# Quarter products for the forget-gate and value projections inside the gated scan

## The chip, the cores and the metric

The kernel runs on one core of a Trainium2 chip. The metric is the device time of one execution in microseconds (us), the median over runs. TensorE is called PE here, VectorE DVE, ScalarE ACT, GpSimd POOL; SP is the engine whose queue issues most of the transfers.

## The reference, cut to what matters

Two transformer blocks run one after the other. The second one (the suffix `_2` in the weights) projects 256 context tokens and 256 latent tokens with `w_in_2`, runs a gated linear scan over 8 heads in two directions, and attention beside it:

```python
b = jnp.cumsum(log_f, axis=3)                 # in chunks of 32 tokens
k_inv, q_dec = k * jnp.exp(-b), q * jnp.exp(b)
kv_chunk = einsum('bhnsk,bhnsv->bhnkv', k * jnp.exp(b_last - b), v)
S = decay * S + kv_chunk                      # from chunk to chunk
o = tril(q_dec k_inv^T) v + q_dec S
```

A forget gate is a sigmoid of a projection of all 512 tokens by 128 columns of `w_in_2` (one set for each head and each direction), scaled into a lower bound; k is one minus the gate. The value of a head is a projection of all 512 tokens by 128 columns, without a function. Query and output gate are needed for the 256 latent tokens only.

## The kernel before, in words

Everything is float32, and each matmul of the source is two matmul instructions in the trace. The stages that matter are `in_projection2` (the input norm and the projections of heads 0 and 1), `hgrn` (the scan of all heads, and the projections of heads 2 to 7 and of attention beside it), and `attention`.

**Weights** come through a ring of three slots of 2 MB (2048 x 256 columns). SP issues the loads strictly in the order of the list `SLOTS`; load n waits until slot n-3 is given back (`issue`, L338). In `hgrn` nine slots make a group (the slots are counted from the stage's first): f0, mod, f1, mod, q, mod, i, mod, g. f0 and f1 hold the gate columns of the two directions for two heads, i the value columns, and mod is a slice of `w_mod_2`, which DVE, not PE, multiplies (`mod_macs`, L661 to L672: 16 instructions and one add) and gives back at its end. One mod slot is used in each step u = 0 to 13: slots 1, 3, 5, 7, 10, 12, 14, 16, 19 and so on.

**The scan** has 16 steps u (head u//2, direction u%2). In each, PE writes the chunk products (L2835; the moment it starts is called kv(u) below), DVE carries the state through them in 15 dependent instructions (`carry_state`, L3065 and L3067), and PE reads the later states (L2843, then eight times L2848). DVE then forms the sums of step u+1 (L3028 to L3036), ACT their exponentials (L2923 to L2926), DVE the end keys (L3042), then the 16 instructions of `mod_macs`, then the masked scores (L3047), then the gate of the next step (L3021). PE turns the keys of u+1 (L2806) and makes the scores (L2812).

**Dense work beside the scan.** PE fills its gaps with the projections, a generator of jobs (`MIX2_JOBS`) of which `fill(us)` takes as many matmuls as their written prices make up:

```python
MIX2_FILL = {"carry": 7.0, "step": 0.43, "ahead": 11.0, "keys": 5.0}
```

In one step this is 7.0 after kv(u), seven times 0.43 between the reads of the states, 11.0 after them, and 5.0 after the keys: 26.0 us by the written prices. 14.0 us are taken ahead of step 0. After every fourth step what is left of the group is done at once (`fill_upto`). The written price is 0.856 us for a matmul of 512 columns and 0.428 for one of 256. A group p (1 to 3) has four f jobs (16 matmuls of 512 columns, L2752), two q (16 of 256, L2754), four i (16 of 256, tokens on the partitions, L2750) and two g (as q). Jobs alternate between banks 5 and 7; a job may start when ACT has emptied the one before the last (`W("dense_out", j - 1)`). ACT empties them in `dense_out`, at fixed places in its own list: ahead of `log_gates`, ahead of `exponentials`, ahead of `keys_out`.

`in_projection2` already computes its own f0 and f1 as seven quarter products with sums of tokens (`tok_sum`) and of weights (L2594 to L2599) by DVE.

Of the kernel before, what the change touches and what calls it, by code (L numbers as in the profile page):

```python
# [217 lines left out]
MIX2_FILL = {"carry": 7.0, "step": 0.43, "ahead": 11.0, "keys": 5.0}  # L218
# [1645 lines left out]
def ffn(nc, st, name, which, mods, gain, shift):  # L1864
# [58 lines left out]
    with nc.Block() as block:  # L1923
        @block.sync
        def _(sp):
# [3 lines left out]
            if which == 0:  # L1929
                sp.dma_start(st.const[:, st.const_late:], st.dram["const"][:, st.const_late:]).then_inc(st.s_back, 16)  # L1930
# [480 lines left out]
def in_projection2(nc, st):  # L2411
# [13 lines left out]
    s_tokens, s_wsum, s_seven, s_p1, s_post = (st.sem("in2_" + x) for x in ("token_sums", "weight_sums", "products", "p1", "post"))  # L2425
# [22 lines left out]
    with nc.Block() as block:  # L2448
        @block.sync
        def _(sp):  # L2450
            stream_weights(sp, st, SPANS["mix2"][0] + RING)
# [99 lines left out]
        def _(dve):  # L2551
# [36 lines left out]
            tt(tok_sum[3], tok_sum[1], tokens(1, 0), ALU.subtract).then_inc(s_tokens, 1)  # L2588
# [12 lines left out]
            def post(x):  # L2601
# [12 lines left out]
                vl.mark(tt(fb[:, one], fb[:, two], r[4], ALU.subtract))  # L2614
# [9 lines left out]
            for k in range(KT):  # L2624
                x = st.xT[:, k, :]
                vl.mark(stt(x, x, final[:, k:k + 1], ra, ALU.mult, ALU.mult))
# [9 lines left out]

MIX2 = []
for _g in range(4):
    if _g < 3:
        _p = _g + 1  # L2640
        _jobs = [("f", 4 * _p + _u) for _u in (0, 2, 1, 3)] + [("q", 2 * _p), ("q", 2 * _p + 1)]
        _jobs += [("i", 4 * _p + _t) for _t in range(TT)] + [("g", 2 * _p), ("g", 2 * _p + 1)]
        if _g:
            _jobs.insert(2, ("hn", _g - 1))
# [9 lines left out]
def mix2_slot(job):  # L2654

    kind, i = job
    if kind in ("f", "q", "i", "g"):
        p = {"f": i // 4, "q": i // 2, "i": i // 4, "g": i // 2}[kind]
        return 9 * (p - 1) + {"f": 2 * (i % 2), "q": 4, "i": 6, "g": 8}[kind]
    return {"ak": 27, "aq": (29, 31, 32, 33)[min(i // 2, 3)], "av": 34}[kind]  # L2660

# [5 lines left out]
def hgrn(nc, st):  # L2667
# [42 lines left out]
    norms = [("nk", 0), ("nk", 1)] + [("nq", n) for n in range(4)]  # L2710

# [11 lines left out]
    with nc.Block() as block:  # L2723
        @block.sync
        def _(sp):
            stream_weights(sp, st, SPANS["att"][0] + RING)

        @block.tensor
        def _(pe):
# [4 lines left out]

            def dense():
                nonlocal done
                freed = None
                for j, (kind, i) in enumerate(MIX2_JOBS):
# [3 lines left out]
                    if kind in ("f", "q", "i", "g", "ak", "aq", "av"):  # L2742
# [3 lines left out]
                        half = {"f": i // 2 % 2}.get(kind, i % 2)  # L2746
                        for k in range(KT):
                            if kind in ("i", "av"):
                                t = i % 4
                                last = mm(b[:, 0:256], st.h2[:, t // 2, k, (t % 2) * P:(t % 2 + 1) * P], w[:, k, :], start=k == 0, stop=k == KT - 1)  # L2750
                            elif kind in ("f", "ak"):
# [9 lines left out]
                            yield 0.856 if kind in ("f", "ak") else 0.428  # L2761
# [56 lines left out]
            for u in range(U):  # L2818
# [3 lines left out]
                if h >= 2:  # L2822
                    W("dense_out", mix2_at(("i", h // 2 * 4 + 3)))
# [21 lines left out]
                for n in range(8, 16):  # L2845
# [5 lines left out]
                    if n < 15:  # L2851
                        fill(MIX2_FILL["step"], upto=marks[u, "carry"] + 2)
                fill(MIX2_FILL["ahead"], (u, "ahead"))
# [9 lines left out]
        def _(act):  # L2863
# [5 lines left out]
            def dense_out(upto):  # L2869
# [3 lines left out]
                while n_out < upto:  # L2873
# [3 lines left out]
                    if kind == "f":  # L2877
                        W("kend", i // 4 * 4 - 4)
                        W("qk", 2 * (i // 4 * 4 - 4))
                        ins = a_(fu(i), x[:], ACT.Sigmoid)  # L2880
# [3 lines left out]
                    elif kind == "i":  # L2884
                        W("inter", 8 * (i // 4 * 4 - 4))
                        ins = nc.scalar.copy(st.pi[i // 4 % 2][:, i % 4, :], x[:, 0:256])
# [45 lines left out]

            log_gates(0)
# [3 lines left out]
            for u in range(U):  # L2937
# [3 lines left out]
                dense_out(marks[u, "carry"])  # L2941
                if u + 1 < U:
                    exponentials(u + 1)
# [8 lines left out]
                if u + 1 < U:  # L2952
                    keys_out(u + 1)
            dense_out(J)
# [17 lines left out]
        def _(dve):  # L2972
# [44 lines left out]
            def gates(u):  # L3017
                f, lc = fu(u), 8 * (u % 2) + u // 2
                if u >= 4:
                    W("dense_out", mix2_at(("f", u)))  # L3020
# [375 lines left out]
```

## Time and profile before

| what | value |
|---|---|
| median of 3 runs | 3558.76 us |
| the runs | 3560.2, 3549.15, 3558.76 us |
| span of the profiled execution | 3558.3 us |
| PE busy | 96% of the span |
| DVE, ACT, POOL busy | 66%, 16%, 5% |
| `hgrn` in the trace | about 2042 to 2575 us |

The span runs from the first to the last instruction. The profiled execution's time outside the span is not given; the span lies 0.5 us under the median of the runs. "Idle before" is the time for which an engine stood still just ahead of an instruction, with what released it. Busy time of PE counts overlapping records once, and a mean duration includes the drain, so a price is taken from start to start.

### The profile page before, as it was taken

What the parts mean: (1) busy time and instruction counts of PE and PEld (TensorE: products, weight loads), DVE (VectorE), ACT (ScalarE), POOL (GpSimd) and SP (SyncE); (2) the same over time, 40 slices, a digit from 0 to 9 for tenths busy, and PEclk for the clock granted to TensorE, in tenths of its full rate; (3) what the DMA queues carried; (4) which work ended last, traced back from release to release, by engine and by line L of the source; (5) the groups of instructions that cost most, each with busy time, mean ns of one, the idle gap of its engine ahead of it and who ended that gap; (6) DMA issues with size and microseconds to landing.
All of it is one profiled execution on the core that took longest, in us unless ns stands there. A gap on an engine that the chain in (4) does not pass through costs nothing. (4 is left out here: it accounts for less than half of the span.)

```text
span 3558.3 us, 58548 instructions
## 1 busy us (share of the span) xinstructions
PE 3421.8 (96%) x25037; PEld 2759.0 (78%) x25037; DVE 2336.2 (66%) x4471; ACT 564.2 (16%) x1072; POOL 162.7 (5%) x168
## 2 busy tenths in 40 slices
PE   7998999899999999999999999999999999999999
PEld 4456555577778888889998866767877888888888
DVE  2277877785559888998776645555654656644644
ACT  2232222221001000000002132222221000000000
POOL 1000000000000000000001000000001000000000
PEclk9999999999999999999999999999999999999999
DMA  9833333344587878776665644544324676654543
GB/s 338 259 79 105 104 86 106 106 120 122 191 285 234 263 245 267 237 253 203 212 209 182 205 150 142 166 142 132 120 80 147 222 234 201 221 174 160 178 166 130
DMA packets 663410, 638.48 MB, mean 179 GB/s; under 512 B 43490, under 2 KB 630752, under 8 KB 662128
## 3 DMA queue, kind: packets, MB, share of 16 engines
q1 hardware_dynamic: 554464, 563.16, 49.3%
q10 hardware_dynamic: 108016, 71.44, 6.9%
q8 instruction: 198, 3.24, 0.4%
q14 instruction: 60, 0.49, 0.0%
q0 software_dynamic: 672, 0.15, 0.0%
HBM read 628.41 MB, written 6.29 MB: 178 GB/s over the span
## 5 line engine op out<-in xcount | busy, mean ns | idle before, releaser
L2005 PE MATMUL bank<-work,extra 128*128 128x256 f32 x2112 | 463.1, 379 | 0.0
L664 DVE SCALAR_TENSOR_TENSOR work<-weight_ring,silu_c,work 128x256 f32<-128x256 f32 x1050 | 450.5, 501 | 0.0
L2005 PEld LDWEIGHTS bank<-work,extra 128*128 128x128 f32 x2112 | 401.3, 190 | 53.5
L2005 PE MATMUL bank<-weight_ring,work 128*128 128x256 f32 x1408 | 318.1, 385 | 8.1 <-ACT work L2138 7.5
L2206 DVE TENSOR_TENSOR work<-weight_ring 128x2048 f32<-128x2048 f32 (+2 forms) x72 | 129.7, 1801 | 294.1 <-DMA weight_ring<-in_w_gate_up 160.9
L2005 PEld LDWEIGHTS bank<-weight_ring,work 128*128 128x128 f32 x1408 | 269.8, 193 | 45.5 <-issue 8.3
L1013 PE MATMUL bank<-work,x_channels 128*128 128x256 f32 (+1 forms) x704 | 243.5, 486 | 0.0
L2752 PE MATMUL bank<-work,weight_ring 128*128 128x512 f32 x448 | 203.9, 600 | 1.2 <-PEq L2448 1.2
L1013 PEld LDWEIGHTS bank<-work,x_channels 128*128 128x128 f32 x704 | 129.3, 194 | 75.5 <-issue 63.6
L2005 PE MATMUL bank<-weight_ring,extra 128*128 128x256 f32 x704 | 159.3, 380 | 2.2 <-DVE extra L2201 2.2
L2005 PE MATMUL bank<-work 128*128 128x256 f32 x704 | 159.3, 379 | 0.0
L2754 PE MATMUL bank<-work,weight_ring 128*128 128x256 f32 x640 | 151.0, 386 | 0.7 <-ACT work L2899 0.7
L2005 PEld LDWEIGHTS bank<-weight_ring,extra 128*128 128x128 f32 x704 | 133.8, 190 | 20.8 <-issue 2.9
L2752 PEld LDWEIGHTS bank<-work,weight_ring 128*128 128x128 f32 x448 | 81.4, 191 | 86.6 <-issue 84.4
L2217 DVE TENSOR_TENSOR work<-weight_ring,work 128x2048 f32<-128x2048 f32 (+2 forms) x72 | 129.8, 1803 | 27.8 <-PE bank L2005 19.1
L2005 PEld LDWEIGHTS bank<-work 128*128 128x128 f32 x704 | 130.7, 190 | 15.8
L2213 DVE TENSOR_TENSOR work<-work,weight_ring 128x2048 f32<-128x2048 f32 (+2 forms) x72 | 129.4, 1798 | 14.4 <-PE bank L2005 11.4
L2754 PEld LDWEIGHTS bank<-work,weight_ring 128*128 128x128 f32 x640 | 117.8, 190 | 20.9 <-ACT work L2899 4.4
L2209 DVE TENSOR_TENSOR work<-weight_ring 128x2048 f32<-128x2048 f32 (+2 forms) x72 | 129.4, 1797 | 3.4 <-PE bank L2054 2.6
L3067 DVE SCALAR_TENSOR_TENSOR extra<-extra,work,bank 128x128 f32<-128x128 f32 x224 | 77.9, 348 | 78.7 <-PE bank L2848 72.7
L1676 DVE SCALAR_TENSOR_TENSOR const<-weight_ring,silu_c,const 128x256 f32<-128x256 f32 x240 | 116.1, 484 | 18.7 <-DMA weight_ring<-in_w_mod 12.7
L2074 PE MATMUL bank<-work,weight_ring 128*128 128x128 f32 x1056 | 124.6, 276 | 1.7 <-DVE work L2201 1.6
(463 smaller groups left out, 5481.9 us busy)
## 6 DMA issues: line engine op xcount, KB each, us to landing
weight_ring<-in_w_mod SPq DMA_DIRECT2D x80, 2048.0 KB, 9.9
weight_ring<-in_w_gate_up SPq DMA_DIRECT2D x44, 2048.0 KB, 9.4
weight_ring<-in_w_in SPq DMA_DIRECT2D x26, 2048.0 KB, 9.3
weight_ring<-in_w_gate SPq DMA_DIRECT2D x22, 2048.0 KB, 8.3
weight_ring<-in_w_up SPq DMA_DIRECT2D x22, 2048.0 KB, 13.0
weight_ring<-in_w_down SPq DMA_DIRECT2D x20, 2048.0 KB, 8.1
weight_ring<-in_w_mod ACTq DMA_DIRECT2D x32, 1024.0 KB, 6.7
weight_ring<-in_w_out SPq DMA_DIRECT2D x16, 2048.0 KB, 10.2
```

The source lines that it names most:

```text
L664: ins = v_.scalar_tensor_tensor(a, w[:, k, :], c, a, ALU.mult, ALU.add)
L1013: last = mm(b[:, 0:TA if both else T], w[:, k, :], x, start=k == 0, stop=k == KT - 1, skip_group_check=j == 0)
L1676: ins = v_.scalar_tensor_tensor(acc, mod_half[:, k, :], x, acc, ALU.mult, ALU.add)
L2005: last = mm(product(u, p), right[p][:, k, :], left[p][:, k, :], start=k == 0, stop=k == 7)
L2074: last = mm(product2(u, p), left[p][:, k, :], right[p][:, k, :], start=s == 0 and k == 0 and j % 4 == 0, stop=s == 3 and k == hi - lo - 1, ...
L2206: tt(out[0], a21, a22, ALU.add).then_inc(st.s_sum, 1)
L2209: tt(out[1], a11, a21, ALU.subtract).then_inc(st.s_sum, 1)
L2213: tt(out[2], out[0], a11, ALU.subtract).then_inc(st.s_sum, 1)
L2217: tt(out[3], a12, out[2], ALU.subtract).then_inc(st.s_sum, 1)
L2752: last = mm(pair(b[:]), w[:, k, half * P:(half + 1) * P], st.h2[:, :, k, :], start=k == 0, stop=k == KT - 1)
L2754: last = mm(b[:, 0:T], w[:, k, half * P:(half + 1) * P], st.h2[:, 1, k, :], start=k == 0, stop=k == KT - 1)
L3067: v_.scalar_tensor_tensor(where(n + 1), where(n), D[:, u % 2, g:g + 1], kv, ALU.mult, ALU.add).then_inc(S("state"), 1)
```

## The change

The f0, f1 and i slots of groups 1 to 3 (nine slots) are computed as seven products of quarters: the 2048 input channels are halved, and so are the columns (the two heads) and the tokens (context, latent). Each product is 8 matmuls of 256 columns for f (56 a slot, where there were 32 of 512) and 16 of 128 columns for i (112 a slot, where there were 64 of 256). They accumulate in PSUM in the turn 1, 2, 6, 7, 5, 4, 3; ACT empties the bank after each, and DVE adds three kept quarters (`seven_post`). DVE makes four sums of weight quarters a slot, two of them in place in the ring slot (`seven_sums`, `seven_last_sum`). The sigmoid of three of the four quarters is taken later (`open_gates`).

The sums of tokens that the products need are kept from `in_projection2`. Two of them are copied into the place of the residual `xT`, which is written to DRAM before (2 MB) and read back near the end of `hgrn`. So the 16 instructions that scale the residual (L2626) move ahead of the first weight sums, and SP in `in_projection2` waits for the write. A late part of the constants (0.59 MB), loaded at the start of the first feed-forward stage before, is loaded late in `hgrn`. The fill after the states is 9.5 instead of 11.0 in steps 0 to 11, and the limit on the fills between the states goes.

```diff
-MIX2_FILL = {"carry": 7.0, "step": 0.43, "ahead": 11.0, "keys": 5.0}
+MIX2_FILL = {"carry": 7.0, "step": 0.43, "ahead": 9.5, "late": 11.0, "keys": 5.0}
# ffn, SP
-            if which == 0:
-                sp.dma_start(st.const[:, st.const_late:], ...).then_inc(st.s_back, 16)
# in_projection2, SP
+            stream_weights(sp, st, first + 5)
+            sp.wait_ge(s_final, KT)
+            sp.dma_start(st.x_kept, st.xT...).then_inc(st.s_kept, 16)
+            sp.wait_ge(s_tokens, 4)
+            sp.wait_ge(st.s_kept, 32)
+            for j in range(2):
+                sp.dma_start(st.ts_kept[2 + j]..., tok_sum[2 + j]...).then_inc(st.s_tokens_kept, 16)
             stream_weights(sp, st, SPANS["mix2"][0] + RING)
# in_projection2, DVE, ahead of weight_sums(2)
+            for k in range(KT):
+                x = st.xT[:, k, :]
+                stt(x, x, final[:, k:k + 1], ra, ALU.mult, ALU.mult).then_inc(s_final, 1)
# jobs of a group
-        _jobs = [("f", 4 * _p + _u) for _u in (0, 2, 1, 3)] + [("q", 2 * _p), ("q", 2 * _p + 1)]
-        _jobs += [("i", 4 * _p + _t) for _t in range(TT)] + [("g", 2 * _p), ("g", 2 * _p + 1)]
+        _jobs = _seven[0] + ([("hn", _g - 1)] if _g else []) + _seven[1] + [("q", 2 * _p), ("q", 2 * _p + 1)]
+        _jobs += _seven[2] + [("g", 2 * _p), ("g", 2 * _p + 1)]
# hgrn, SP
+            stream_weights(sp, st, first + 28)
+            sp.wait_ge(S("dense_mm"), seven_at(len(SEVENS) - 1, 3))
+            sp.dma_start(st.const[:, st.const_late:], ...).then_inc(st.s_back, 16)
+            sp.dma_start(st.xT..., st.x_kept).then_inc(st.s_x_home, 16)
# hgrn, PE
+            def seven_product(i, b):
+                s, j = i // 7, i % 7
+                p = SEVEN_TURN[j]
...
+                if p == 6:
+                    W("weight_sums", 4 * s + 3)
+                    pe.wait_ge(st.s_tokens_kept, 32)
+                if p == 3:
+                    W("weight_sums", 4 * s + 4)
...
+                if SEVENS[s][1] != "i":
+                    for k in range(8):
+                        yield mm(out, left[:, k, :], right[:, k, :], ...), k == 7, 0.432
+                    return
+                for t in range(2):
+                    for k in range(8):
+                        yield (mm(out[:, t * P:t * P + P], right[:, k, t * P:t * P + P], left[:, k, :], ...), k + t == 8, 0.224)
# hgrn, DVE
+            def seven_sums(s):
+                a11, a12, a21, a22 = quads(s)
+                arrived(dve, st, first + mix2_slot(("s", 7 * s)))
+                if s:
+                    W("dense_mm", seven_at(s - 1, 5))
+                tt(s1, a21, a22, ALU.add).then_inc(S("weight_sums"), 1)
+                tt(a21, a11, a21, ALU.subtract).then_inc(S("weight_sums"), 1)
+                W("weight_sums", 4 * s + 1)
+                tt(s2, s1, a11, ALU.subtract).then_inc(S("weight_sums"), 1)
...
             gates(0)
             sums(0)
             end_keys(0)
+            seven(marks[-1, "ahead"], 0)
             scores_out(0)
             for u in range(U):
                 if u + 1 < U:
                     gates(u + 1)
+                seven(marks[u, "steps"], marks[u - 1, "keys"])
                 carry_state(u)
                 if u + 1 < U:
                     sums(u + 1)
                     end_keys(u + 1)
+                    seven(marks[u, "ahead"], marks[u, "steps"])
                     if u < MIX2_MODS:
                         mod_macs(...)
                     scores_out(u + 1)
+                    seven(marks[u, "keys"], marks[u, "ahead"] - 1)
+                    if u == 12:
+                        dve.wait_ge(st.s_back, 32)
# hgrn, ACT: a further dense_out(marks[u, "steps"]) ahead of exponentials(u + 1), and
+                if u in (2, 6, 10):
+                    open_gates(u // 4 + 1)
# attention, DVE, ahead of the first use of xT
+                    dve.wait_ge(st.s_x_home, 16)
```

`seven(begun, reached)` makes the three sums of a slot as soon as its product 6 is at most three jobs behind `begun`, the last sum by the same rule for product 3, and the three additions once product 4 is at or below `reached`; `marks` are the numbers of jobs that PE has finished at a point of its list.

## Rows read from the trace of the kernel before

**Rows 1.** The page: the span, and busy us (share) and instructions by engine.
```profile
span 3558.3 us, 58548 instructions
PE 3421.8 (96%) x25037; PEld 2759.0 (78%) x25037; DVE 2336.2 (66%) x4471; ACT 564.2 (16%) x1072; POOL 162.7 (5%) x168
```
**Rows 2.** Windows: stretch, length, then busy us (instructions) by engine, clock, DMA share, GB/s.
```profile
1932.00:1936.00 4.00, 4.00 (x11) 3.11 (x10) 3.50 (x9) 4.00 (x12) 3.92 (x1) 0.50 0.00 0
2042.00:2575.00 533.00, 530.84 (x2646) 381.21 (x2646) 298.66 (x635) 152.97 (x244) 40.61 (x48) 1.00 0.44 142
```
**Rows 3.** Groups by line, 2042 to 2575 us: busy us, mean ns, idle before.
```profile
L2752 PE MATMUL bank<-work,weight_ring 128*128 128x512 f32 x448 | 203.9, 600 | 1.2 <-PEq L2448 1.2
```
**Rows 4.** Timeline of PE: start, us, line, operands, count; 256-, 512- and 128-column runs.
```profile
1972.39 13.98 PE L2471 MATMUL bank<-work 128*128 128x256 f32 x64
1986.20 0.50 PE L690 MATMUL bank<-const 128*128 128x1 f32 x4
...
2042.73 13.11 PE L2752 MATMUL bank<-work,weight_ring 128*128 128x512 f32 x30 [1.20 <-PEq L2448]
2055.68 0.60 PE L2806 MATMUL bank<-const,work 128*128 128x128 f32 x4
...
1632.44 5.52 PE L2074 MATMUL bank<-work 128*128 128x128 f32 x48
1637.80 2.84 PE L2074 MATMUL bank<-work,weight_ring 128*128 128x128 f32 x24
```
**Rows 5.** Timeline of DVE in `in_projection2`.
```profile
1961.38 1.22 DVE L2594 TENSOR_TENSOR work<-weight_ring 128x1024 f32<-128x1024 f32 x1
...
1964.90 1.23 DVE L2599 TENSOR_TENSOR work<-weight_ring,work 128x1024 f32<-128x1024 f32 x1
...
1972.23 0.43 DVE L672 TENSOR_TENSOR const<-const 128x256 f32<-128x256 f32 x1
1981.95 1.22 DVE L2594 TENSOR_TENSOR work<-weight_ring 128x1024 f32<-128x1024 f32 x1 [9.29 <-DMA weight_ring<-in_w_in]
...
...
2002.37 6.41 DVE L2626 SCALAR_TENSOR_TENSOR x_channels<-x_channels,params,work 128x256 f32<-128x256 f32 x16
```
**Rows 6.** Timeline of SP: load issues in `in_projection2` and `hgrn`.
```profile
1972.68 0.37 SPq L349 DMA_DIRECT2D weight_ring<-in_w_in  x1
...
2111.60 0.37 SPq L349 DMA_DIRECT2D weight_ring<-in_w_in  x1
...
2142.82 13.48 SPq L349 DMA_DIRECT2D weight_ring<-in_w_in  x2
```
**Rows 7.** DMA issues by line, 2040 to 2600 us: count, KB, median us to landing.
```profile
weight_ring<-in_w_in SPq DMA_DIRECT2D x20, 2048.0 KB, 8.6
```
**Rows 8.** Timeline of PE in `hgrn`: kv(1), kv(2), the state reads (first row: `in_projection2`).
```profile
1986.57 7.15 PE L2471 MATMUL bank<-work,weight_ring 128*128 128x256 f32 x32
...
2088.55 1.17 PE L2835 MATMUL bank<-work,extra 32*128 32x128 f32 x32
2119.55 1.17 PE L2835 MATMUL bank<-work,extra 32*128 32x128 f32 x32
2127.67 0.61 PE L2843 MATMUL bank<-extra,work 128*128 128x128 f32 x4
```
**Rows 9.** Timelines of `hgrn`: end keys, state carry, PE's long fill, ACT behind the exponentials.
```profile
2048.52 0.69 DVE L3042 TENSOR_TENSOR work<-work 128x512 f32<-128x512 f32 x1 [1.49 <-ACT work L2926]
2276.34 3.80 DVE L3067 SCALAR_TENSOR_TENSOR extra<-extra,work,bank 128x128 f32<-128x128 f32 x10
...
2257.41 11.47 PE L2750 MATMUL bank<-weight_ring,work 128*128 128x256 f32 x52
2259.60 1.28 ACT L2883 ACT_TABLE_LOAD   x1
2260.89 0.38 ACT L2883 ACTIVATE work<-bank 128x256 f32<-128x256 f32 x1
```
**Rows 10.** Timeline of PE where it starts again after an idle time.
```profile
1930.24 8.26 PE L2495 MATMUL bank<-weight_ring,work 128*128 128x256 f32 x24 [4.53 <-ACT work L2532]
```

More of the change, by code:

```diff
@@ L2613, in post @@
                 vl.mark(tt(fa[:, two], fa[:, two], r[3], ALU.add))
-                vl.mark(tt(fb[:, one], fb[:, two], r[4], ALU.subtract))
+                vl.mark(tt(fb[:, one], fb[:, two], r[4], ALU.add))
                 vl.wait()
@@ L2634, in _ @@
             side.collect(dve)
+SEVEN_TURN = (1, 2, 6, 7, 5, 4, 3)
+SEVENS = [(p, kind) for p in (1, 2, 3) for kind in ("f0", "f1", "i")]
 MIX2 = []
@@ L2741, in dense @@
                     b = bank[5 + 2 * (j % 2)]
-                    if kind in ("f", "q", "i", "g", "ak", "aq", "av"):
+                    if kind == "s":
+                        s = mix2_slot((kind, i))
+                        arrived(pe, st, first + s)
+                        for last, end, took in seven_product(i, b):
+                            if freed is not None:
+                                last.then_inc(st.s_slot_used, 1)
+                                freed = None
+                            if end:
+                                last.then_inc(S("dense_mm"), 1)
+                                done = j + 1
+                            yield took
+                        if i % 7 == 6:
+                            freed = s
+                    elif kind in ("q", "g", "ak", "aq", "av"):
                         s = mix2_slot((kind, i))
@@ L2851, in _ @@
                     if n < 15:
-                        fill(MIX2_FILL["step"], upto=marks[u, "carry"] + 2)
-                fill(MIX2_FILL["ahead"], (u, "ahead"))
+                        fill(MIX2_FILL["step"])
+                marks[u, "steps"] = done
+                fill(MIX2_FILL["ahead" if u < 12 else "late"], (u, "ahead"))
                 if u % 4 == 3:
@@ L2931, in keys_out, with open_gates @@
                 nc.scalar.copy(keT, bank[4][:].rearrange("p (a b) -> p a b", a=TT)).then_inc(S("keT_out"), 1)
+            def open_gates(p):
+                for s in (3 * p - 3, 3 * p - 2):
+                    W("post", s + 1)
+                    x = quarter(s, 0, 0)
+                    a_(x, x, ACT.Sigmoid)
+                    x = st.pf[p % 2][:, 2 + s % 3, :]
+                    a_(x, x, ACT.Sigmoid).then_inc(S("opened"), 1)
+            act.wait_ge(st.s_tokens_kept, 32)
             log_gates(0)
@@ L2941, in _ @@
                 dense_out(marks[u, "carry"])
+                dense_out(marks[u, "steps"])
                 if u + 1 < U:
@@ L3313, in program @@
         st.c = c
+        st.const_span = lambda name, n: st.const[:, const_where[name][0]:const_where[name][0] + n]
         def carve(at, *shape):
@@ L3333, in program @@
         st.lbs = carve(29120, 4, 16)
+        kept_x = st.xT.rearrange("p k t -> p (k t)")
+        st.ts_kept = [x.rearrange("p (a b) -> p a b", a=8) for x in (
+            st.work[:, 16384:18432], st.work[:, 18432:20480], kept_x[:, 0:2048], kept_x[:, 2048:4096])]
         st.squares = st.extra[:, 3072:4096].rearrange("p (m f t) -> p m f t", m=2, f=2)
```

120 lines of the change are left out of this document (92 added, 28 removed).

## The prediction

> **What bounds the kernel now.** I read the page first: PE is busy for 3421.8 of 3558.3 us, so what shortens PE's list shortens the kernel unless a wait takes its place [rows 1]. The windows then tell where the change lies: from 2042 to 2575 us PE is busy for 530.8 of 533 us at full clock, DVE for 298.7 and ACT for 153.0, and the transfers use 44% of the DMA engines [rows 2]. The stage is PE's, without a gap that matters; the two others have room, but the room is worth something only at the right moment. The groups by line name the work: the gate products alone are 448 instructions of 512 columns (224 matmuls), with 1.2 us idle ahead of them [rows 3]. The last view is the timeline, for what a sum of busy time doesn't show: when each slot is given back, when its successor lands, and when PE asks for it.
>
> **Prices.** From start to start an instruction of 256 columns takes 13.81/64 = 0.2158 us, so a matmul 0.4316; of 512 columns 12.95/30 = 0.4317, so 0.863; of 128 columns 5.36/48 = 0.1117, so 0.2233 [rows 4].
>
> **1. What PE saves.** Six f slots: 32 x 0.863 = 27.6 before, 56 x 0.4316 = 24.2 after, 3.4 each, 20.7 in all. Three i slots: 64 x 0.4316 = 27.6 before, 112 x 0.2233 = 25.0 after, 2.6 each, 7.8. Sum **-28.5 us**. The 128-column rows come from a stream in which every instruction has its own load of 128x128 weights, as in the new i product, so I take that price as it is. Its bounds are near: half of the 256-column price below (24.2 us a slot, 0.8 less), and the price of 256 columns above, which the rival on weight loads takes up.
>
> The Trainium skill speaks against the i half. Its page "TensorE: Matmul & The Clock Gate", section "Back-to-back issue gap", says that in a stream of weight loads and matmuls the spacing at 128 columns is set by both, about 81 ns where 56 would be the stream alone, a factor of 1.45. By that rule the i slot would cost 224 x 0.1079 x 1.45 = 35.0 us (estimate), and the sum would be 30 us worse. The trace disagrees: 0.1117 is 1.04 times half of 0.2158 [rows 4].
>
> **2. What DVE gets.** Three sums of 128x1024 take 3.5 us from 1961.38 to 1964.90 [rows 5]; with the fourth and three additions of some 0.4 it is 5.8 us a slot, 52 in nine. DVE has 234 us free in the stage [rows 2], so the amount is hidden. Where it stands is not: three places below.
>
> **3. in_projection2.** The 16 scalings (6.4 us, L2626) move ahead of weight_sums(2). PE asks for sum 5 at 1972.4 and the sum would be ready at 1969.0, so that is hidden. But the mod slot behind it is given back 6.4 us later, and SP issued load first+4 on that release, at 1972.68 [rows 5, 6]. It landed at 1981.95, 9.3 us later; now 1988.4, and PE asks at 1986.57 [rows 8]: **+1.9**. SP then waits for the write of the residual, and the two copies and loads first+5 and first+6 queue behind it. By 8.6 us for 2 MB [rows 7] in a row, first+6 lands at some 2014: 1992.7 for the write, then three times 2 MB at 6.5 to 8.6; PE asks at 2013, seven products of 3.45 behind 1988.5. If everything stands in line at 8.6, it is 6 us late. I take **+1.0**, range 0 to 6. The reload and the constants late in the stage lie behind the last i slot and are asked for 25 us later: 0, and up to 2 if they push load 29. Taking the constants out of the first feed-forward stage gains nothing that a wait of PE shows.
>
> **4. Start of hgrn.** PE starts at 2042.73 and has products 1 and 2 done at 2049.7. Product 6 needs three sums, which DVE puts after end_keys(0), ending at 2049.2 [rows 9]; they end at 2052.7: **+3.0**. In step 0 the sums of the second slot wait for product 5 of the first, which PE does 4 us after kv(0), and they stand ahead of carry_state(0): they end at +7.7, the eighth state is there at +10.7 (8 x 0.38 [rows 9]), and PE asks at 8.1 + 0.6 = +8.7 [rows 8]: **+2.0**.
>
> **5. The slot that PE reaches too early.** This is the step that decides. Slot 6 (i) follows mod slot 3 in the ring, which DVE gives back at the end of mod_macs(1): SP issued it at 2111.60, kv(1) + 23.05 [rows 6, 8]. Before, PE came to it late enough: by written prices 14 + 2 x 26 = 66 us are taken ahead of kv(2), and 4 x 13.7 + 13.7 = 68.5 lie ahead of i. After, a step takes 24.51 us, 63.0 ahead of kv(2), and 14 x 3.456 + 13.7 = 62.1 lie ahead of i: PE comes to it 0.9 us before the end of step 1's fill. Step 1 is 31.0 - 1.5 (ahead) - 0.3 (512-column matmuls ran 1% over their written price) = 29.2 long, 0.5 of its end are the four modulation columns (as the four of [rows 4]), so PE asks at kv(1) + 27.8. DVE's additions push mod_macs(1) by 1.1, the load is issued at +24.2 and lands at +32.8: **+5.0**. Queued behind it is everything PE does in step 2. The same for slot 8 (g), on mod slot 5: issued at 2142.82, kv(2) + 23.3, now 24.4 with one sum ahead, landing at +33.0. Work ahead of g is 62.1 + 25.1 = 87.2 of 87.5 taken, so PE asks at 29.2 - 0.8 = +28.4: **+4.6**. In group 2 the i slot lands at kv(6) + 3.9 with PE asking at +3.3, and DVE's sums for it stand ahead of carry_state(6): +1.8; in group 3 the same, +0.5; **+2.3**. The other slots land 5 us or more ahead.
>
> **6. Clock.** PE started again at 1930.24 after 4.5 us idle, and a window of 4 us behind it had clock 0.50; its 24 instructions took 8.1 us where 5.2 is their price [rows 2, 10]. The two waits of 5 us are near to that one: half speed for 4 us is 2.0 each (the rest of the 2.9 I put down to input that was still arriving), **+4.0**. The range is 0, if the clock holds, to 6.
>
> **Sum.** -28.5 + 1.9 + 1.0 + 3.0 + 2.0 + 5.0 + 4.6 + 2.3 + 4.0 = -4.7 us. Against the span, 3558.3 - 4.7 = 3553.6; the median of the runs lies 0.5 above the span, so **3554.1 us**, 0.13% under 3558.76. What a measurement can tell from no change is about 0.3%, 10.7 us.
>
> **Rivals.**
> *Most of the gain arrives* (3540 us, chance 0.30). If the loads land in 6 us, not 8.6, the two waits are 2.5 us shorter each, and if the clock stays full another 4 go: -4.7 - 5 - 4 = -13.7, and 3558.8 - 13.7 = 3545; with the start and step 0 hidden too, 3540. For it: PE's work falls by 28.5 whatever else happens. Against it: the median landing is 8.6 [rows 7].
> *ACT becomes the bound, slower* (3572 us, chance 0.13). A quarter job takes 8 x 0.4316 = 3.45 us, where an f job took 13.8, and PE may only be one job ahead of ACT. After the reads of the states ACT is held by the exponentials: PE's long fill began at 2257.4, ACT took the next bank at 2260.9 and was done at 2261.3 [rows 9], 3.9 us. It decides from the point where the hold passes the rest of the job in work plus one, 3.45 to 6.9. If additions and sums ahead of the carry hold DVE by 2.5 us, the hold is 6.4 and PE loses some 1.5 us in each of 12 steps: +18. Against it: the additional dense_out ahead of the exponentials, and few of the sums stand ahead of the carry.
> *Weight loads bound the 128-column products, slower* (chance 0.03). PE would pay for the second load of each pair: at 0.156 us an instruction, 224 a slot, three slots, 30 us more: 3584. The row of 0.1117 at the same shapes is against it [rows 4].
> *The change doesn't act*: the products are fewer by count, so only if the old matmuls were paced by something else than columns; 0.863 against 0.4316 says no. Chance 0.02, 3580 with the waits.
>
> **The numbers.** The likeliest case (waits and gain as summed, -14 to +6) has 0.52. Its own range is 3545 to 3565. Faster by more than 0.3%: the first rival and the lower edge of the likeliest, 0.34. Slower by more: the ACT rival, the weight-load rival and the rest, 0.17. Within: 0.49. The range to hold 8 in 10 reaches down to the first rival (clock 4, half of the two waits 5, the start and step 0 5: 3540, put at 3539) and up to the bounds of 3 and 6 with a third of ACT's price (5 + 2 + 2 + 6: 3569).
>
> **What would show it.** Instructions of 256 and 128 columns in hgrn at 0.216 and 0.112 from start to start. PE idle on the DMA of a weight slot (or a sequencer wait) some 5 us ahead of the first i product of step 1 and the first g product of step 2, with the SP issue right behind the add that ends mod_macs. 3 us of PE idle on DVE some 7 us into hgrn. Steps of 29.2 us from kv to kv elsewhere below step 12. A clock below 1 near steps 1 and 2 only. ACT's releases of PE in total below 5 us. I am wrong if PE's busy time in the stage falls by less than 25 us, if the two slot waits are below 2 us, or if PE waits for ACT in every step.

## The result

The changed kernel takes 3570.38 us, median of 16 runs (3558.32 to 3584.96); the kernel before took 3557.75 on the same chips (16 runs, 3549.15 to 3569.25). The ratio is 1.0033, with a 95% interval of 1.0020 to 1.0045: slower by 12.6 us between the medians, just outside what a measurement can tell from no change. (A ratio is not exactly the quotient of the two medians; differences in us are between medians unless a sentence says otherwise.) Predicted were 3554.1 us, and a range whose upper end (3569) lies 1.4 us below the measured median. The forecast was wrong: it said a small gain, and the change is a small loss.

The page of the changed kernel, where the span and the busy times of the engines answer to [rows 1]:

```profile
span 3573.7 us, 59884 instructions
PE 3410.2 (95%) x25613; PEld 2824.0 (79%) x25613; DVE 2387.0 (67%) x4534; ACT 581.4 (16%) x1123; POOL 162.7 (5%) x168
```

PE is busy for 11.6 us less and the span is 15.4 us longer. The windows of `hgrn` tell more. The first row is the whole stage, from its first PE instruction to the first of `attention`; the others are short stretches in it (length, busy us and count of PE, weight loads, DVE, ACT, POOL, then clock, DMA share, GB/s):

```profile
2050.20:2591.60 541.40, 517.85 (x3222) 448.94 (x3223) 349.35 (x698) 170.18 (x296) 40.63 (x48) 0.97 0.44 145
2062.00:2065.00 3.00, 3.00 (x9) 2.41 (x9) 0.00 (x0) 0.00 (x0) 0.00 (x0) 0.58 0.00 0
2083.00:2086.00 3.00, 3.00 (x10) 2.55 (x10) 1.66 (x5) 0.00 (x0) 0.00 (x0) 0.50 0.00 0
2138.00:2141.00 3.00, 3.00 (x21) 2.98 (x24) 3.00 (x4) 0.00 (x0) 0.00 (x0) 0.50 0.56 165
2141.00:2144.00 3.00, 3.00 (x39) 2.78 (x32) 1.62 (x5) 0.63 (x1) 0.62 (x1) 0.50 1.06 358
2176.00:2180.00 4.00, 4.00 (x40) 3.56 (x39) 0.58 (x2) 0.00 (x0) 0.00 (x0) 0.50 0.55 172
2400.00:2404.00 4.00, 3.49 (x16) 3.50 (x17) 2.41 (x9) 0.00 (x0) 0.00 (x0) 0.55 0.53 173
2404.00:2408.00 4.00, 4.00 (x25) 4.00 (x23) 2.96 (x6) 0.20 (x1) 0.00 (x0) 0.59 0.00 0
2408.00:2412.00 4.00, 4.00 (x38) 4.00 (x38) 1.28 (x3) 3.00 (x7) 1.65 (x2) 1.00 0.01 4
```

Cut the same way, the stage took 532.5 us before at clock 1.00 (530.84 of them busy, [rows 2]); now it takes 541.4. PE is busy for 517.85, so for 23.5 us it is idle, and in five places it works at clock 0.50, PE's lower level of 1.2 GHz. The last two rows show what that does: in the four microseconds from 2404 it does 25 instructions, in the four behind them 38. A window's length times (1 - clock), summed over windows of 5 us through the stage, is the time that the low clock cost: **13.6 us**, and none before.

The waits of PE from 2040 to 2600 us (waiting line, releaser, us in total, times, longest):

```profile
PE bank L2915 <- DVE extra L3198: 7.7, 3, 4.5
PE bank L2785 <- DMA weight_ring<-in_w_in: 4.9, 1, 4.9
PE bank L2820 <- DMA weight_ring<-in_w_in: 4.8, 1, 4.8
PE bank L2781 <- DVE const L3110: 4.2, 1, 4.2
PE bank L2781 <- PEq L2446: 1.4, 1, 1.4
PE bank L3280 <- PEq L2750: 0.9, 1, 0.9
PE bank L2820 <- ACT work L2976: 0.7, 1, 0.7
PE bank L690 <- DVE const L672: 0.7, 1, 0.7
PE bank L2781 <- ACT work L2960: 0.2, 1, 0.2
```

The first four lines are new, 21.6 us in six waits. Their places are in the timeline of PE, start and duration first:

```profile
2061.55 5.38 PE L2781 MATMUL bank<-work,const 128*128 128x256 f32 x16 [4.20 <-DVE const L3110]
2066.76 1.89 PE L2781 MATMUL bank<-x_channels,weight_ring 128*128 128x256 f32 x8
2068.49 0.60 PE L2872 MATMUL bank<-const,work 128*128 128x128 f32 x4
...
2082.56 0.41 PE L2915 MATMUL bank<-work,extra 128*128 128x32 f32 x2 [2.21 <-DVE extra L3198]
...
2137.50 2.39 PE L2785 MATMUL bank<-weight_ring,work 128*128 128x128 f32 x10 [4.90 <-DMA weight_ring<-in_w_in]
...
2175.46 1.19 PE L2820 MATMUL bank<-work,weight_ring 128*128 128x256 f32 x2 [4.79 <-DMA weight_ring<-in_w_in]
...
2400.51 0.64 PE L2915 MATMUL bank<-work,extra 128*128 128x32 f32 x2 [4.52 <-DVE extra L3198]
2400.95 1.20 PE L2785 MATMUL bank<-weight_ring,work 128*128 128x128 f32 x4
...
2407.97 0.69 PE L2785 MATMUL bank<-weight_ring,work 128*128 128x128 f32 x4
...
2415.20 3.07 PE L2785 MATMUL bank<-weight_ring,x_channels 128*128 128x128 f32 x26
2418.10 0.60 PE L2872 MATMUL bank<-const,work 128*128 128x128 f32 x4
```

They stand at the start (sums of the first slot), in step 0 (carry behind the second slot's sums), at the first i product of step 1, at the first g product of step 2, and in step 10. The four 128-column instructions at 2400.95 take 1.20 us, and the same four at 2407.97 take 0.69: half speed, then full. The prices at full speed are as forecast: 1.73/8 = 0.216 us for 256 columns (2066.76 to 2068.49) and 2.90/26 = 0.1115 for 128 (2415.20 to 2418.10).

The stages (first PE instruction to first PE instruction of the next): `in_projection2` 112.5 before, 115.8 after, +3.3; `hgrn` +8.9; `attention` with the output projection 151.7 and 151.6; the last feed-forward stage 824.9 and 824.0. So +12.2 us lie in the two stages that the change touches, and 12.6 were measured. Of the 15.4 between the two profiled spans another 4.2 lie ahead of `in_projection2`, nearly all of them in the `rwkv` stage (779.4 and 783.5 us), which the change does not touch (see e12 below).

### The profile page after: what moved, and what is told of

The parts are those of the page before. It is cut to its first block and busy times, and to the rows that moved or that the text cites. A ratio compares the mean times of both kernels' runs of the same rounds, so it can differ in the third digit from the quotient of the medians.

```text
span 3573.7 us, 59884 instructions
## 1 busy us (share of the span) xinstructions
PE 3410.2 (95%) x25613; PEld 2824.0 (79%) x25613; DVE 2387.0 (67%) x4534; ACT 581.4 (16%) x1123; POOL 162.7 (5%) x168
## 5 line engine op out<-in xcount | busy, mean ns | idle before, releaser
L2820 PEld LDWEIGHTS bank<-work,weight_ring 128*128 128x128 f32 x640 | 118.1, 192 | 24.7 <-issue 6.1
L2143 ACT ACTIVATE work<-extra 128x512 f32<-128x512 f32 x44 | 27.7, 630 | 590.2 <-DVE extra L2262 590.2
L1013 PE MATMUL bank<-work,extra 128*128 128x256 f32 (+1 forms) x342 | 119.8, 489 | 3.3 <-ACT work L1381 1.6
## 6 DMA issues: line engine op xcount, KB each, us to landing
weight_ring<-in_w_up SPq DMA_DIRECT2D x22, 2048.0 KB, 12.6
```

Source lines behind the costliest of these rows:

```text
L1013: last = mm(b[:, 0:TA if both else T], w[:, k, :], x, start=k == 0, stop=k == KT - 1, skip_group_check=j == 0)
L2820: last = mm(b[:, 0:T], w[:, k, half * P:(half + 1) * P], st.h2[:, 1, k, :], start=k == 0, stop=k == KT - 1)
```

## The experiments

All ratios are to the kernel before, run on the same chip. An experiment stays near the median of the changed kernel if its edit does nothing: ratio 1.0033.

**e1: PE is given work in two of the waits.** Ten matmuls of 256 columns into the bank that the job is about to start afresh, 4.3 us, ahead of the first i job of group 1 and the first g job:

```diff
+                    if (kind, i) in (("s", 14), ("g", 2)):
+                        for _ in range(10):
+                            mm(b[:, 0:256], st.h2[:, 1, 0, 0:P], st.h2[:, 1, 1, :], start=True, stop=True, ...)
```

> The changed kernel with ten more matmuls of 256 columns (4.3 us, their result is overwritten and the output is the reference's) just ahead of the first i product and of the first g product of group 1, where PE idles for 4.9 and 4.8 us on a weight slot and its clock is then 0.50 for 6.8 us each. Theory (the idle time costs twice, in the wait and in the lower clock behind it): the waits shrink to about 0.6 and 0.5 us, filled by the added work, the two stretches of 0.50 are gone, and the kernel is 6 to 7 us faster than the changed one (3570 to about 3564), though PE does more. Rival (the lower clock costs nothing that counts, or comes from something else): no gain, and up to 1 us slower.

Measured: 3565.77 us (12 runs), ratio 1.0015 (1.0005 to 1.0026), `hgrn` 534.9 us. The windows of e1 in these two places:

```profile
2132.00:2136.00 4.00, 3.84 (x55) 3.71 (x56) 3.86 (x4) 0.00 (x0) 0.00 (x0) 1.00 0.57 180
2167.00:2171.00 4.00, 3.77 (x46) 3.40 (x47) 1.42 (x5) 0.00 (x0) 0.00 (x0) 1.00 0.49 146
```

The waits were 0.5 and 0.7 us, and the clock stayed at 1.00. PE's list grew by 8.6 us and the two waits shrank by 8.5, and yet the three steps around them took 34.3, 34.4 and 29.8 us from kv to kv instead of 35.7, 36.8 and 32.0: 6.0 us less, for 6.8 that the windows of the changed kernel put down to the low clock at these two places. Elsewhere in `hgrn` the changes cancel but for half a microsecond (a shorter wait at the start, 2.5; longer low clock behind step 10's). `in_projection2`, where e1 has the changed kernel's code, took 118.1 us in this profile instead of 115.8, with a low stretch of its own; so the stage, and not the medians (their intervals overlap), carries the reading. To do useless work cost less than to wait.

**e2: the sums of the first slot first.**

```diff
             gates(0)
+            seven(marks[-1, "ahead"], 0)
             sums(0)
             end_keys(0)
-            seven(marks[-1, "ahead"], 0)
```

> The changed kernel with DVE's first three weight sums in hgrn ahead of sums(0) and end_keys(0), not behind. Theory: the wait of 4.2 us of PE on the sum (L3110) goes, and the stretch of 3.4 us at clock 0.50 behind it, 5 to 6 us faster than the changed kernel (about 3565). Rival (the chain of the scan decides there, and its keys come 3.5 us later): the wait moves to the first turn of the keys (L2872), no change.

Measured: 3568.24 us (12 runs), 1.0023 (1.0009 to 1.0036), `hgrn` 540.1: 2 us faster than the changed kernel where 5 to 6 were forecast. The wait of 4.2 us went (from the stage's start to kv(0) 16.9 us instead of 21.4), but step 0 became 36.5 us instead of 33.2. Its wait was the same, 2.2 us; what followed was not:

```profile
2073.00:2077.00 4.00, 4.00 (x13) 3.39 (x13) 2.10 (x4) 0.00 (x0) 0.00 (x0) 0.50 0.00 0
2077.00:2081.00 4.00, 4.00 (x14) 3.44 (x13) 1.52 (x4) 0.73 (x2) 0.00 (x0) 0.50 0.00 0
```

These eight microseconds lie in a stretch of about ten at 0.50 behind 2.2 us of waiting, where the changed kernel had three. The low clock cost 17.1 us in this stage (13.6 before the edit). Whether the edit or the execution made the stretch longer, one profile cannot tell.

**e3 and e12: the rest of the change with the old products.** The kernel before, with the write of the residual, the copies of the token sums, the earlier scalings, and the reload and constants at the end of `hgrn`; e12 is the same program again.

```diff
+            sp.wait_ge(s_final, KT)
+            sp.dma_start(st.x_kept, st.xT...)
...
-                vl.mark(stt(x, x, final[:, k:k + 1], ra, ALU.mult, ALU.mult))   # now ahead of weight_sums(2)
...
+            sp.wait_ge(S("dense_mm"), mix2_at(("i", 15)))
+            sp.dma_start(st.const[:, st.const_late:], ...)
+            sp.dma_start(st.xT..., st.x_kept)
```

> The kernel before, products as they were, with all else of the change around them: the scalings of the residual ahead of the first weight sums, the write of the residual, the copies of two sums of tokens into its place, the reload and the late constants, and the waits of SP, ACT and DVE that go with them. Theory: +3.3 us against before (what in_projection2 took longer, 112.5 to 115.8 us), so about 3561, and nothing in hgrn. Rival (the transfers also disturb the loads of hgrn, the reload above all): +6 or more, with waits of PE for slots late in hgrn.

Measured: 3571.82 us (12 runs), 1.0027 (1.0013 to 1.0041). `in_projection2` took 118.0 us (+5.5: waits for slots of 0.9 and 2.1, and 3 us at low clock behind the second), `hgrn` 532.5, step by step as before. The reload and the constants at its end cost nothing. But the interval (+4.6 to +14.6) holds these 5.5 only near its lower end, and the profile had another 10 in `rwkv`, which no edit touches:

```profile
164.10:954.00 789.90, 714.95 (x10711) 487.35 (x10712) 573.79 (x1328) 197.87 (x374) 0.93 (x1) 0.95 0.39 107
```

Before, that stage took 779.4 us with the same 10711 PE instructions. So the same program was run again:

> The same program as e3_spill_only, for one question: is the length of the rwkv stage, which no edit of this study touches, a property of the program or of the execution? In the profiles it was 779.4 us in the kernel before and 789.9 in e3_spill_only, which is 10.5 of the 12.4 us by which the medians differ beyond the 5.5 found in in_projection2 and nothing in hgrn. Theory P (the program's: another layout of its code or data slows the stage): 788 to 792 us again. Theory X (the execution's: its low-clock stretches fall differently each time): some other value between 775 and 787. hgrn 532.5 and in_projection2 116 to 119 under both. Median of the runs 3567 to 3575 if the 12 runs of e3_spill_only were typical.

Measured: 3565.55 us (8 runs), 1.0014 (0.9995 to 1.0034); `rwkv` 779.6, `in_projection2` 117.5, `hgrn` 534.2 (low clock just behind its start). The 10 us do not belong to the program. Nor do they follow the chip, as far as the other profiles show: on the chip of e3 the stage took about 777, 776 and 778 us in e1, e2 and e4. Over all 14 profiles it ranges from about 776 to 790 us. A difference of this size can account for much of the scatter of some +-10 us in the runs of every version (no other runs were taken apart by stage), so the stages are better compared than the spans. The cost in `in_projection2` differs too: with the scalings ahead it took 115.7 to 118.1 us in seven profiles, 3.2 to 5.6 more than before.

**e4: less work behind the states,** so that PE comes later to each slot.

```diff
-MIX2_FILL = {"carry": 7.0, "step": 0.43, "ahead": 9.5, "late": 11.0, "keys": 5.0}
+MIX2_FILL = {"carry": 7.0, "step": 0.43, "ahead": 7.8, "late": 11.0, "keys": 5.0}
```

> The changed kernel with 7.8 instead of 9.5 us of dense work behind the state reads in steps 0 to 11; the same work in all, the rest is done behind each fourth step. Theory (PE reaches the slots of i and g before their load has landed, since a load is issued only when the mod slot ahead of it is given back, once a step): i is reached 3.3 us into step 2, where the load lands at about 5.4, g at 5.8 of step 3 where it lands at 5.9; the wait of 4.8 and its low clock go, that of 4.9 falls to 2 to 3, and the waits of 1.0 and 4.5 in steps 6 and 10 go with their low clock: 15 to 19 us faster than the changed kernel, 3552 to 3556, under the kernel before. Rival (the loss is a price of the short products and their emptying by ACT, or of DVE's extra work): within 3 us of the changed kernel.

Measured: 3547.32 us (12 runs), 0.9972 (0.9955 to 0.9989), `hgrn` 516.5. The waits for weight slots shrank from 9.7 to 1.1 us, the one in step 10 went, those at the start and in step 0 stayed (2.5 and 2.2), and two low stretches of about 3 us remained, at the stage's start and in step 0. One number turns the loss of 12.6 us into a gain of 12 (10 by the ratio), more than the forecast.

**e5: the scalings back behind the weight sums,** so that the mod slot is given back as early as before.

```diff
@@ ahead of weight_sums(2)
-            for k in range(KT):
-                x = st.xT[:, k, :]
-                stt(x, x, final[:, k:k + 1], ra, ALU.mult, ALU.mult).then_inc(s_final, 1)
...
@@ behind side.accumulate(dve, first + 3)
+            for k in range(KT):
+                x = st.xT[:, k, :]
+                stt(x, x, final[:, k:k + 1], ra, ALU.mult, ALU.mult).then_inc(s_final, 1)
```

> The changed kernel with the 16 scalings of the residual behind the multiplication of the first mod slot, where DVE idled 8.6 us, instead of ahead of the first weight sums. Theory (the scalings delay the release of that slot and so the load of f1 by 6.4 us, and the spill queues ahead of q's load): in_projection2 falls from 115.8 to 112.5 to 113.5 us, no wait on f1's slot, the wait of 1.7 on q's slot shorter; 2 to 3 us faster than the changed kernel in the median. Rival (what the spill costs is its transfers, wherever the scalings stand): in_projection2 stays above 115 us.

Measured: 3566.83 us (12 runs), 1.0026 (1.0013 to 1.0039). `in_projection2` was back at 112.9 us, without a wait for a slot; `hgrn` was 542.4, with the waits of the changed kernel.

**e6: the first sums first, and those of the second slot kept off the carry of step 0.** The edit of e2, and:

```diff
-            def seven(begun, reached):
+            def seven(begun, reached, made=99):
...
+                          and (summed[0] == 0 or seven_at(summed[0] - 1, 5) <= made)):
...
-                seven(marks[u, "steps"], marks[u - 1, "keys"])
+                seven(marks[u, "steps"], marks[u - 1, "keys"], marks[u - 1, "keys"])
```

> The changed kernel with the first weight sums ahead of sums(0), as in the run before, and the second slot's sums in step 0 put behind the state's carry when they would have to wait for a product of that step. Theory: both waits (4.2 and 2.2 us) and both low-clock stretches near them go; kv(0) comes 4.5 us earlier, step 0 takes 29 to 30 us instead of 33.2, hgrn 8 to 9 us shorter (541.4 to about 533), where the first sums alone gave 1.3 because the other wait then drew a longer stretch of low clock. Rival (the sums are needed so early that PE waits for them behind the carry instead): step 0 stays above 32.

Measured: 3563.48 us (12 runs), 1.0015 (0.9997 to 1.0032), `hgrn` 535.6, step 0 at 30.2 us. Both waits went (one of 1.0 us came in step 0), but each of the two slot waits was now followed by about 10 us of low clock instead of 7:

```profile
2134.00:2138.00 4.00, 4.00 (x43) 3.76 (x42) 2.57 (x6) 0.63 (x1) 0.62 (x1) 0.50 1.03 336
2138.00:2142.00 4.00, 4.00 (x26) 4.00 (x25) 2.98 (x10) 0.37 (x1) 0.00 (x0) 0.65 0.53 168
```

**e7: e5 and e6, with 7.0 behind the states.**

```diff
-MIX2_FILL = {"carry": 7.0, "step": 0.43, "ahead": 9.5, ...}
+MIX2_FILL = {"carry": 7.0, "step": 0.43, "ahead": 7.0, ...}
```

> The changed kernel with all repairs: the scalings later, the sums of the two last kernels, and 7.0 us of dense work behind the state reads in steps 0 to 11. Theory: no wait of PE on a weight slot, a sum or a state above 1.5 us and no clock below 1 in hgrn after its start; hgrn at 506 to 510 us (541.4 in the changed kernel, 516.5 with 7.8 alone), in_projection2 at 113; about 3539 to 3544 us, 0.4 to 0.6% under the kernel before. Rival (the repairs move the waits, since with less dense work a step DVE and the loads fall behind elsewhere): above 3547.

Measured: 3544.37 us (11 runs), 0.9957 (0.9941 to 0.9974), `hgrn` 516.2. The slots were no longer waited for, but with less to do PE now reached DVE's results too early: 1.8 us on the scores and 2.5 on the states, with 6.8 us of low clock behind the second. The forecast of 506 to 510 us for `hgrn` failed: 7.0 is too little.

**e8: the kernel before with 7.8.** The control: is it the shorter fill alone?

```diff
-MIX2_FILL = {"carry": 7.0, "step": 0.43, "ahead": 11.0, "keys": 5.0}
+MIX2_FILL = {"carry": 7.0, "step": 0.43, "ahead": 7.8, "keys": 5.0}
```

> The kernel before with 7.8 instead of 11.0 us of dense work behind the state reads, nothing else. It tells whether the smaller fill is a gain by itself. Theory: the kernel before has no wait for a slot in hgrn, so the same work only moves behind each fourth step; hgrn stays at 532.5 us and the median within 3 us. Rival (shorter steps are better in any case): 5 us or more faster.

Measured: 3558.26 us (12 runs), 0.9994 (0.9980 to 1.0007), `hgrn` 532.9. It only moves work into every fourth step (47.0 us instead of 33.2 in step 7).

**e9 and e13: e5 and e6 with 7.8,** and the same program again.

```diff
-MIX2_FILL = {"carry": 7.0, "step": 0.43, "ahead": 9.5, ...}
+MIX2_FILL = {"carry": 7.0, "step": 0.43, "ahead": 7.8, ...}
```

> As the kernel with all repairs, but 7.8 instead of 7.0 us of dense work behind the state reads in steps 0 to 11. With 7.0 two waits of 1.8 and 2.5 us came up in steps 0 and 2 with 6.8 us of low clock. Theory (the step was so short that DVE came late with the scores of step 1, at kv(0) + 27, and with the sums ahead of the carry of step 2): with steps 0.8 us longer the wait for the scores falls from 1.8 to about 1, that of step 2 stays near 1 to 2; hgrn 510 to 514 us (516.2 with 7.0), the median 3538 to 3544. Rival (at this size the waits do not depend on the fill): hgrn at 516.

Measured: 3536.65 us (6 runs), 0.9929 (0.9910 to 0.9948): 22 us faster than the kernel before (25 by the ratio), some 34 than the changed one. `in_projection2` took 112.8 us. The window of its `hgrn` as a whole, and its five longest waits:

```profile
2041.60:2552.20 510.60, 505.95 (x3222) 438.83 (x3223) 347.39 (x698) 168.69 (x295) 40.95 (x48) 1.00 0.47 153
```

```profile
PE bank L2781 <- PEq L2446: 1.3, 1, 1.3
PE bank L2781 <- DVE const L3110: 1.0, 1, 1.0
PE bank L2915 <- DVE extra L3199: 0.9, 1, 0.9
PE bank L3281 <- PEq L2750: 0.9, 1, 0.9
PE bank L2785 <- DMA weight_ring<-in_w_in: 0.8, 1, 0.8
```

The same 3222 instructions as in the changed kernel, 30.8 us sooner: no wait is longer than 1.3 us, and the clock is at full speed but for one short stretch at the start.

> The same program as e9_together_7_8, beside e12_spill_again on the same chip. Its hgrn stage was 510.6 us, its rwkv stage 779.9. Theory P (the rwkv length belongs to the program): 778 to 782 us again. Theory X (it belongs to the execution): anything from 775 to 791. hgrn: 509 to 514 us if the short waits that are left (1.0, 0.8, 0.9 us) draw no low clock or one stretch of 3 us; up to 517 if they draw two or three. Median 3533 to 3545.

Measured: 3542.28 us (4 runs), 0.9941 (0.9904 to 0.9978); `hgrn` 511.9 with waits of 0.6 to 1.3 us, 5.0 in all, and no low stretch; `rwkv` 785.8, where e9 had 779.9.

**e11: e9 with the i slots as before,** that is, with six slots as quarter products (the waits, the copies by ACT and the sigmoids that go with them are not shown).

```diff
-SEVENS = [(p, kind) for p in (1, 2, 3) for kind in ("f0", "f1", "i")]
+SEVENS = [(p, kind) for p in (1, 2, 3) for kind in ("f0", "f1")]
...
-        _jobs += _seven[2] + [("g", 2 * _p), ("g", 2 * _p + 1)]
+        _jobs += [("i", 4 * _p + _t) for _t in range(TT)] + [("g", 2 * _p), ("g", 2 * _p + 1)]
```

> The kernel of the run beside it with the value slots (i) as in the kernel before, four jobs of 16 matmuls of 256 columns on each of three slots, and seven products for the gate slots only. It gives the price of the products with 128 columns. Theory (0.112 us an instruction from start to start): PE's work is 7.8 us more, the waits on i's sums in step 2 are gone (1 to 3 us), hgrn 5 to 8 us longer than in the run beside it. Rival (a weight load for each 128 columns costs what the rule of the Trainium skill says, or the extra sums eat it): hgrn shorter or equal without the i part.

Measured: 3547.78 us (9 runs), 0.9965 (0.9951 to 0.9979); `hgrn` 517.0, 6.4 more than e9 and 5.1 more than e13. The i half is worth 5 to 6.4 us where 7.8 were summed. The medians of e11 and e9 differ by 11.1; what makes the rest of it is not shown (the profile of e11 had `rwkv` at 790.4 us against 779.9, but one execution says little on a median).

**All stages by one sum.** If step 1 of the prediction holds, every version's `hgrn` is 532.5 - 28.5 = 504.0 us (511.8 for e11), plus its new waits, plus what the low clock cost (window lengths times 1 - clock):

| version | new waits | low clock | other | sum | `hgrn` | rest |
|---|---|---|---|---|---|---|
| changed | 21.6 | 13.6 | | 539.2 | 541.4 | 2.2 |
| e1 | 11.3 | 8.5 | 8.6 | 532.4 | 534.9 | 2.5 |
| e2 | 17.5 | 17.1 | | 538.6 | 540.1 | 1.5 |
| e4 | 6.8 | 3.4 | | 514.2 | 516.5 | 2.3 |
| e5 | 21.8 | 15.4 | | 541.2 | 542.4 | 1.2 |
| e6 | 16.1 | 15.4 | | 535.5 | 535.6 | 0.1 |
| e7 | 4.3 | 5.1 | | 513.4 | 516.2 | 2.8 |
| e9 | 2.7 | 1.4 | | 508.1 | 510.6 | 2.5 |
| e13 | 5.0 | 0 | | 509.0 | 511.9 | 2.9 |
| e11 | 1.7 | 1.7 | | 515.2 | 517.0 | 1.8 |

"Other" is the added work of e1. In e1, e2, e4, e6, e7, e9 and e11 the low clock includes 1.4 to 1.7 us at the very start of the stage, which e8 and e12 have too, with the old products. Three terms account for the stage in ten versions to within 3 us: what the change saves was there all the time, 25 to 28 us of it, and what stood against it are waits and the clock behind them.

## Why the prediction was wrong

**The step that failed is 6, the clock.** It allowed half speed behind the two longest waits only, 4 us each, and took 4.0 us, at most 6, from one stretch of the trace before [rows 10]. Measured were 13.6: all five places with waits of 2.2 us and more had a low stretch, of about 3, 3, 7, 7 and 7 us. That is 9.6 of the 16.5 us by which `hgrn` came out longer than forecast (+8.9 instead of -7.6). e1 isolates it: with the waits at two places filled by as much useless work, 6.0 us came back.

The trace before had both things that the forecast missed. Its window of 4 us lay inside a longer stretch, and a wait of 2.0 us just ahead (PE started again at 1922.11) had a stretch of about 3 us behind it:

```profile
1923.00:1925.00 2.00, 2.00 (x6) 1.63 (x5) 0.74 (x4) 0.00 (x0) 0.00 (x0) 0.50 0.90 286
1930.00:1936.00 6.00, 5.76 (x14) 4.63 (x15) 5.50 (x14) 6.00 (x17) 3.92 (x1) 0.50 0.00 0
```

PE worked 5.76 us at half speed there, which costs 2.9 us: the whole 2.9 of the forecast's own row, of which it put 0.9 down to input that was still arriving. That a low stretch costs half its length is also what the Trainium skill states ("TensorE: Matmul & The Clock Gate", section "HAM oscillation — how this bites in real kernels", a penalty of the throttled time times 1 - 1.2/2.4); the trace agrees: the sixteen instructions of 256 columns from 2061.55 took 5.2 us from start to start where 3.45 is their price, 1.7 us more, with 3.4 us of low clock in them.

**Steps 4 and 5, the waits in `hgrn`: right in their places, 21.6 us for 16.9.** At the start 4.2 for 3.0, in step 0 2.2 for 2.0, at the i slot 4.9 for 5.0, at the g slot 4.8 for 4.6, group 2 1.0 for 1.8. The i slot's load is issued behind the add that ends `mod_macs(1)`, at kv(1) + 24.6 where +24.2 was forecast:

```profile
2125.69 3.24 DVE L664 SCALAR_TENSOR_TENSOR work<-weight_ring,silu_c,work 128x256 f32<-128x256 f32 x8
2128.97 0.42 DVE L672 TENSOR_TENSOR work<-work 128x256 f32<-128x256 f32 x1
```

```profile
2129.42 0.37 SPq L349 DMA_DIRECT2D weight_ring<-in_w_in  x1
```

It lands 8.1 us later, at 2137.50. The term mis-sized here is group 3, 4.5 instead of 0.5: DVE waited for the i slot until kv(10) + 6.7, and its three sums stood ahead of the carry:

```profile
2394.07 1.22 DVE L3107 TENSOR_TENSOR work<-weight_ring 128x1024 f32<-128x1024 f32 x1 [5.40 <-DMA weight_ring<-in_w_in]
2395.22 1.22 DVE L3108 TENSOR_TENSOR weight_ring<-weight_ring 128x1024 f32<-128x1024 f32 x1
2396.35 1.22 DVE L3110 TENSOR_TENSOR const<-work,weight_ring 128x1024 f32<-128x1024 f32 x1
2397.49 0.28 DVE L3196 COPY extra<-bank 128x128 f32<-128x128 f32 x1
2397.80 3.41 DVE L3198 SCALAR_TENSOR_TENSOR extra<-extra,work,bank 128x128 f32<-128x128 f32 x9
```

The forecast had these sums ahead of the carry too, but gave group 3 "the same" as group 2, where the slot was to land at kv(6) + 3.9 (measured: + 3.5). The load of group 3 was issued in time, at kv(9) + 23.5, and landed 12.5 us later, not 8.6. SP had issued another 2 MB only 3.1 us before it; ahead of group 2's i slot that was 7.6 us, and the landing took 8.2:

```profile
2378.53 0.37 SPq L349 DMA_DIRECT2D weight_ring<-in_w_mod  x1
2381.60 0.37 SPq L349 DMA_DIRECT2D weight_ring<-in_w_in  x1
```

That the two loads shared the transfer time is the likely cause; no run tried it.

So waits 4.7, clock 9.6 and the rest of 2.2 in the table are the 16.5.

**Step 3, `in_projection2`: right.** +3.3 us for +2.9, in waits of 0.9 and 1.7 for slots; e5, which puts the scalings back, takes 2.9 of it away. In four of the seven profiles with this code a low stretch behind the second wait added 1.7 us (e1, e2, e3, e12); the forecast had no such term.

**Step 1, PE's saving: right, slightly high.** The table's rest says 25.6 to 28.4 for 28.5 (e9 and e13: 26.0 and 25.6). My own test for it, that PE's busy time fall by 25 us, was badly chosen: it fell by 13.0 only (530.84 to 517.85), since an instruction is busy for longer at half clock (25 instructions in 4 us from 2404, 38 in the next 4). In e9, at full clock, it fell by 24.9. Steps without a wait took 29.4 to 29.8 us from kv to kv, where 29.2 were forecast.

**Step 2, DVE's sums: hidden in amount, as said.** DVE is busy for 349.35 us instead of 298.66, 50.7 more for 52. Their places cost the waits at the start and in step 0 (e2 and e6 take them away) and, with the late slot, those in steps 6 and 10.

**The rivals.** "ACT becomes the bound" is refuted: ACT released PE for 0.9 us in the stage. So is "weight loads bound the 128-column products": 0.1115 us an instruction, and e11 shows the i half worth 5 to 6.4 us. "Most of the gain arrives" is what e9 does, but by other edits than a faster landing. The measured case, slower by the forecast's own waits with a clock price of 13.6 us where its bound was 6, was not among the rivals; it should have been, with step 10's wait as its second half.

**Left open.** Why the same wait of 2.2 us is followed by 3 us of low clock in one profile and by 7 or 10 in another; since each version has one profile (two for e3 and e9, by e12 and e13), an edit and an execution can't be told apart there. What sets the time from issue to landing (8.1 to 12.5 us here) was not tried. Of the 0.1 to 2.9 us of rest in the table no cause was looked for.

## What to carry to other kernels

When PE's list becomes shorter, ask for every buffer when PE *and* the engines that prepare its operands will now ask for it, and shift the filling work (here one number, 9.5 to 7.8) until no wait is longer than about a microsecond: a gain of 25 to 28 us was there in PE's list and came out as +12.6, or as -22 us (-17 when run again), by that and by where three groups of DVE instructions stand (the scalings and the sums of the first two slots). Price a wait in an otherwise full PE stage at its length plus the low clock behind it: here 21.6 us of waits cost 35. And compare stages rather than spans where an unchanged stage moves by 10 us between executions of one program.

## What the runs showed of the hardware

- A wait of 2.2 us in a stage that was full on either side was followed by a stretch at 0.50 in all five versions that had it in step 0 (the changed kernel, e1, e2, e4, e5), for about 3, 3, 10, 3 and 7 us. The fifteen waits of 4.2 to 5.0 us in `hgrn` in these versions and e6 all were. The waits of 2.5 us near the start of `hgrn` (e1, e4) were not, nor the one of 1.8 us in e7, nor the waits of 0.6 to 1.3 us inside the stage.
- Whether a short wait draws such a stretch differs from execution to execution. Behind the second slot wait of `in_projection2` (1.6 to 2.3 us) it came in four of seven profiles with the same code of that stage. At the start of `hgrn`, behind waits of 0.9 to 1.7 us with one of 0.4 to 1.0 just before, it came in nine of fourteen profiles; of two profiles of one program e12 had it and e3 had not, and so had e9 and had not e13.
- One such stretch cost between 1.7 and 5.1 us, at times more than the wait itself. Behind the same wait it was not always as long: behind the two slot waits it was about 7 us in the changed kernel and 10 in e6, and behind the wait of 4.5 us in step 10 it was 7, 10 (e1) and 3 (e5).
- A stage with the same instructions took 789.9 and 779.6 us in two executions of one program (e3, e12), at clock 0.95 and 0.96.
